# The last norm before the experts: its factors applied to the queries' scores, the queries fed from the unscaled residual

## The reference, cut to what matters

```python
h = h + hybrid_mixer(...)                      # ends in a product with w_out_2
hn = rms_norm(h, ffn_norm_2)                   # h * rsqrt(mean(h*h) + 1e-6) * gain
q = (hn @ w_query).reshape(t, 8, 2, 128)       # 8 heads, two halves of 128
scores = einsum('thcd,hckd->thck', q, sub_keys)
top_s, top_i = top_k(scores, 16)               # then the 16 best sums of 16 x 16, softmax as gates
# experts: gelu(hn . expert_down[idx]), gated, times expert_up[idx]
```

## Time and profile before

| | |
|---|---|
| time of three executions | 3069.96, 3070.07, 3074.51 us; median 3070.07 |
| the profiled execution | 3074.27 us, span 3071.2 us |
| PE busy | 3027.9 us (99%) |
| DVE busy | 2314.5 us (75%) |
| ACT busy | 1672.5 us (54%) |
| POOL busy | 476.7 us (16%) |
| mean granted TensorE clock | 0.996 of 2.4 GHz |
| units split by DVE | 1030, mean 1223 ns |

### The profile page before, as it was taken

One profiled execution on the slowest core, in us unless ns is written; L12 is line 12 of the kernel. 1 busy time (PEld: TensorE's weight loads), 2 busy tenths in 40 slices (PEclk: granted clock), 3 DMA queues, 4 the chain that ended last, 5 costly groups with the idle time before them and its releaser, 6 DMA issues.

```text
span 3071.2 us, 44079 instructions
## 1 busy us (share of the span) xinstructions
PE 3027.9 (99%) x17646; PEld 2695.9 (88%) x17646; DVE 2314.5 (75%) x3465; ACT 1672.5 (54%) x2469; POOL 476.7 (16%) x316
## 2 busy tenths in 40 slices
PE   8999999999999999999999999999999999999999
PEld 7999988888888888889897789999999988888887
DVE  5477667777776455567766589999998898999987
ACT  5454555444444345454564545599975555555544
POOL 1000000000000000000000000133323323775551
PEclk9999999999999999999999999999999999999999
DMA  6543455556555655655344656788889999999997
GB/s 219 187 159 124 143 166 178 186 186 187 186 188 188 197 189 189 188 171 175 117 138 145 202 173 218 256 287 294 287 312 352 357 353 354 402 396 383 392 382 261
DMA packets 199211, 726.79 MB, mean 237 GB/s; under 512 B 22240, under 2 KB 22368, under 8 KB 198496
## 3 DMA queue, kind: packets, MB, share of 16 engines
q1 hardware_dynamic: 161280, 585.44, 56.1%
q0 software_dynamic: 37360, 136.79, 12.2%
q10 hardware_dynamic: 368, 1.75, 0.2%
HBM read 719.24 MB, written 4.19 MB: 236 GB/s over the span
## 4 chain that ended last, share of the span: by engine, by line
PE 91%; DVE 5%; DMA 2%; ACT 2%; issue 1%; ACTq 0%; SPq 0%; DVEq 0%
PE b L2097 90%; DVE wlo L1253 2%; DMA raw<-in_dn 2%; PE b L2105 1%; DVE ar L1242 1%; ACT oh L629 1%; ACT ar L629 0%; ACT whi L633 0%; DVE ar L1831 0%; DVE ar L1823 0%; DVE ar L1818 0%; DVE ar L1815 0%; DVE ar L1826 0%; DMA hsb<-in_x 0%; DVE hsb L2005 0%
## 5 line engine op out<-in xcount | busy, mean ns | idle before, releaser
L1253 DVE TENSOR_TENSOR wlo<-raw,whi 128x1024 fp32r<-128x1024 f32 x1030 | 1252.4, 1223 | 498.5 <-ACT whi L633 494.3
L2097 PE MATMUL b<-aa,whi 128*128 128x256 f32 (+2 forms) x6080 | 1614.2, 343 | 3.7 <-DVE wlo L1253 3.7
L633 ACT ACTIVATE whi<-raw 128x1024 fp32r<-128x1024 f32 x1030 | 1076.3, 1055 | 680.1 <-DMA raw<-in_up 182.1
L2097 PE MATMUL b<-aa,wlo 128*128 128x256 f32 (+1 forms) x4896 | 1280.1, 269 | 0.0
L2097 PEld LDWEIGHTS b<-aa,whi 128*128 128x128 f32 x6080 | 1056.1, 190 | 85.2 <-issue 13.6
L2097 PEld LDWEIGHTS b<-aa,wlo 128*128 128x128 f32 x4896 | 929.7, 190 | 9.8
L2097 PE MATMUL b<-whi,asb 128*128 128x512 f32 x1092 | 366.2, 389 | 2.2 <-DVE ex L1242 2.2
L2097 PE MATMUL b<-whi,aa 128*128 128x512 f32 x1024 | 324.7, 394 | 5.6 <-DVE aa L1250 3.7
L619 POOL DMA_INDIRECT aaf<-in_up,ex x128 | 271.2, 2119 | 161.3 <-DVE aaf L1250 157.9
L2097 PE MATMUL b<-wlo,asb 128*128 128x512 f32 x728 | 283.2, 389 | 0.0
L608 POOL DMA_INDIRECT hsb<-in_dnr,ex x128 | 183.3, 1432 | 464.8 <-DVE small L2005 454.7
(11 more groups left out here) (183 smaller groups left out, 2707.0 us busy)
## 6 DMA issues: line engine op xcount, KB each, us to landing
raw<-in_dn SPq DMA_DIRECT2D x256, 512.0 KB
raw<-in_up SPq DMA_DIRECT2D x182, 512.0 KB
raw<-in_wgu SPq DMA_DIRECT2D x176, 512.0 KB
raw<-in_wdn SPq DMA_DIRECT2D x88, 512.0 KB
raw<-in_w1fm SPq DMA_DIRECT2D x74, 512.0 KB
raw<-in_w2fm SPq DMA_DIRECT2D x74, 512.0 KB
raw<-in_wo SPq DMA_DIRECT2D x64, 512.0 KB
hsb<-in_up SPq DMA_DIRECT2D x44, 512.0 KB, 7.4
```

The source lines that it names most:

```text
L633: return e.activation(o, i, ACT.Copy)
L1253: return e.tensor_tensor(o, a, high.bitcast(F32), ALU.subtract)
L2097: return e.matmul(o, l, r, start=start, stop=stop)
```

## The change

The early flips, highs and lows of the unscaled residual go behind units of the last half of `WO2`, into arrays `PARTS` of their own; the other four groups stand between `WO2` and `WQ`. The last four squares, the factors, the scaling into `XN`, its transposes and its split become a task `renorm` that runs in the ticks of `WQ` and writes `AH`, `AL` for tokens 64 to 255 alone. The factors are applied when ACT copies the scores, as two instructions of 256 columns with a scale in place of one of 512. The queries' scores use two PSUM banks in place of four. The load of `GR` is issued at the end of the task.

The diff, eight columns of indent cut, with the body of the three removed `norm()` left out:

```diff
--- before.py
+++ after.py
@@ -183,7 +183,8 @@
-TURNED = [[4, 5, 6, 7, 4, 5, 6, 7], [6, 7, 5, 1, 2, 0, 3, 4], [4, 5, 6, 7, 0, 1, 2, 3], [0, 1, 2, 3, 4, 5, 6, 7]]
+TURNED = [[4, 5, 6, 7, 4, 5, 6, 7], [6, 7, 5, 1, 2, 0, 3, 4], [4, 5, 6, 7, 0, 1, 2, 3], [0, 1, 2, 3, 4, 5, 6, 7],
+  [5, 6, 7, 3, 5, 6, 7, 3]]
@@ -374,7 +375,8 @@
-    GR = AGf[0:64, 10240:12288]
+    GR = AGf[0:64, 0:2048]
+    JK5 = AGf[:, 3584:4096]
@@ -410,6 +412,16 @@
+with ExitStack() as ph:
+    q15, _, qa, _, qb = [sb(f"parts{i}", n, FR, ph) for i, n in enumerate((3584, 6656, 5632, 8704, 2048))]
+    PARTS = [a[:, i * 512:(i + 1) * 512] for a, n in ((qa, 11), (qb, 4)) for i in range(n)] + [q15[:, 3072:3584]]
+    PARTS = [a.rearrange("p (s t) -> p s t", s=2) for a in PARTS]
+def parts(m, k):
+    return PARTS[k] if m == 4 else AA[:, :, k, :]
@@ -426,6 +438,8 @@
+w_x, w_y, w_p, w_ah, w_al = [sem(f"w_{k}") for k in ("x", "y", "p", "ah", "al")]
@@ -663,7 +677,7 @@
-            act(AH[:, k, :], B[TURNED[m][g]][:, (k % 2) * 256:(k % 2) * 256 + 256], ACT.Copy,
+            act(parts(m, k)[:, 0, :], B[TURNED[m][g]][:, (k % 2) * 256:(k % 2) * 256 + 256], ACT.Copy,
@@ -685,26 +699,33 @@
-    def norm():
+    def renorm():
+        for i, (t, c) in enumerate(((0, 2), (1, 2), (0, 3), (1, 3))):
+            e.wait_ge(s_add, 40)
+            e.wait_ge(n_sq, 36 + i)
+            square(JK5, h[:, t, hcol(c)], t, c).then_inc(n_sq, 1)
+            if i % 2:
+                yield
...
+        yield
+        for n in range(25):
+            c, g = n // 6, n // 3 - 1
+            if n % 6 == 0 and c < 4:
+                e.wait_ge(n_v, NV[4] + 6)
+                if c == 3:
+                    e.wait_ge(w_p, 2)
+                act(XN[:, c % 3, 1, :], h[:, 1, hcol(c)], ACT.Copy, scale=small[:, 13:14]).then_inc(w_y, 1)
+            if n % 3 == 0 and g >= 0:
+                e.wait_ge(w_p, g + 1)
+                e.wait_ge(s_u, U["WQ"])
+                for k in (2 * g, 2 * g + 1):
+                    o = (k % 2) * 256
+                    act(AH[:, k, TS:256], B[6 + g % 2][:, o + TS:o + 256], ACT.Copy,
+                        scale=col(GAIN[4], k)).then_inc(w_ah, 1)
+            yield
+        e.wait_ge(s_sk, 16)
+        e.wait_ge(w_p, 8)
+        e.dma_start(GR, g5).then_inc(s_sk, 16)
@@ -1106,14 +1127,15 @@
-         lambda ch, t, c, u: add_h(33 + 4 * ch + 2 * c + t, t, 2 * ch + c, B[BANKS[15 + ch][2 * c + t]]))
+         lambda ch, t, c, u: None if ch else add_h(33 + 2 * c + t, t, c, JK5),
+         lambda ch, n: high(4, n - 7) if ch and 7 <= n < 11 else None)
-    e.wait_ge(n_sq, 40)
-    e.dma_start(GR, g5).then_inc(s_sk, 16)
-    norm()
+    for g in range(4, 8):
+        high(4, g)
+    tasks.add(renorm())
@@ -1121,7 +1143,11 @@
-        cp(SCS[:, :, hd * 256:(hd + 1) * 256], B[4 + hd % 4].rearrange("p (t w) -> p t w", t=2)).then_inc(s_sc, 1)
+        e.wait_ge(n_v, NV[4] + 6)
+        for t in range(2):
+            last = act(SCS[:, t, hd * 256:(hd + 1) * 256], B[4 + hd % 2][:, t * 256:(t + 1) * 256], ACT.Copy,
+                       scale=small[:, 12 + t:13 + t])
+        last.then_inc(s_sc, 1)
@@ -1291,8 +1317,9 @@
-            stt(AL[:, k, :], B[bank][:, (k % 2) * 256:(k % 2) * 256 + 256], col(GAIN[m], k),
-                AH[:, k, :].bitcast(F32), ALU.mult, ALU.subtract).then_inc(n_al, 1)
+            p = parts(m, k)
+            stt(p[:, 1, :], B[bank][:, (k % 2) * 256:(k % 2) * 256 + 256], col(GAIN[m], k),
+                p[:, 0, :].bitcast(F32), ALU.mult, ALU.subtract).then_inc(n_al, 1)
@@ -1310,23 +1337,25 @@
-    def norm():
+    def renorm():
+        yield
+        yield
...
+        yield
+        for n in range(25):
+            c, g = n // 6, n // 3 - 1
+            if n % 6 == 0 and c < 4:
+                e.wait_ge(n_v, NV[4] + 6)
+                if c == 3:
+                    e.wait_ge(w_p, 2)
+                ts(XN[:, c % 3, 0, :], h[:, 0, hcol(c)], small[:, 12:13], None, ALU.mult).then_inc(w_x, 1)
+            if n % 3 == 0 and g >= 0:
+                e.wait_ge(w_ah, 2 * g + 2)
+                for k in (2 * g, 2 * g + 1):
+                    o = (k % 2) * 256
+                    stt(AL[:, k, TS:256], B[6 + g % 2][:, o + TS:o + 256], col(GAIN[4], k),
+                        AH[:, k, TS:256].bitcast(F32), ALU.mult, ALU.subtract).then_inc(w_al, 1)
+            yield
@@ -1794,11 +1823,14 @@
-    rows(U["WO2"] + 8, order2[4:16], 2, tasks, need2, unit, lambda ch, t, c, u: add(15 + ch, t, 2 * ch + c, u))
+    rows(U["WO2"] + 8, order2[4:16], 2, tasks, need2, unit, lambda ch, t, c, u: add(15 + ch, t, 2 * ch + c, u),
+         lambda ch, n: low_parts(4, n - 7) if ch and 7 <= n < 11 else None)
-    norm()
+    for g in range(4, 8):
+        low_parts(4, g)
+    tasks.add(renorm())
@@ -1878,7 +1910,7 @@
-    e.wait_ge(n_a, 14)
+    e.wait_ge(w_y, 4)
@@ -2119,8 +2151,12 @@
+        elif m == 3:
+            e.wait_ge(s_pv, 8 if g < 4 else 12 if g < 6 else 16)
-            e.wait_ge(s_pv, 8 if g < 4 else 12 if g < 6 else 16)
+            e.wait_ge(s_add, 36 if g < 4 else 38 if g < 6 else 40)
+            if g >= 4:
+                e.wait_ge(n_al, 64 + 2 * g - 6)
@@ -2138,17 +2174,23 @@
-    def norm():
...
+    def renorm():
+        for n in range(27):
+            g = (n - 5) // 3
+            if n >= 5 and n % 3 == 2:
+                if g % 2 == 0:
+                    e.wait_ge(w_x, g // 2 + 1)
+                    e.wait_ge(w_y, g // 2 + 1)
+                e.wait_ge(n_al, 80)
+                if g >= 2:
+                    e.wait_ge(w_al, 2 * g - 2)
+                for k in (2 * g, 2 * g + 1):
+                    for t in range(2):
+                        o = (k % 2) * 256 + t * 128
+                        last = tr(B[6 + g % 2][:, o:o + 128],
+                                  XN[:, g // 2 % 3, t, (k % 4) * 128:(k % 4 + 1) * 128])
+                last.then_inc(w_p, 1)
+            yield
@@ -2176,11 +2218,12 @@
+                p = parts(m, k)
-                    mm(b, hi, AA[:, :, k, :], k == 0, False)
-                last = mm(b[:, 0:256], lo, AH[:, k, :], False, False)
+                    mm(b, hi, p, k == 0, False)
+                last = mm(b[:, 0:256], lo, p[:, 0, :], False, False)
-                    last = mm(b, hi, AA[:, :, k, :], False, True)
+                    last = mm(b, hi, p, False, True)
@@ -2560,28 +2603,32 @@
-                      lambda ch, j, n=n: wo2_free(8 * n + 4 * ch + j)), nothing)
+                      lambda ch, j, n=n: wo2_free(8 * n + 4 * ch + j)), nothing,
+             early(4, 4) if n else None)
-    norm()
+    for g in range(4, 8):
+        flip(4, g)
+    tasks.add(renorm())
-        e.wait_ge(s_sk, 32)
+        e.wait_ge(s_sk, 16)
-        if hd >= 4:
-            e.wait_ge(s_sc, hd - 3)
+        if hd >= 2:
+            e.wait_ge(s_sc, hd - 1)
-                last = mm(B[4 + hd % 4][:, (2 * t + c) * 128:(2 * t + c + 1) * 128],
+                last = mm(B[4 + hd % 2][:, (2 * t + c) * 128:(2 * t + c + 1) * 128],
-             fm_unit(lambda i: i % 4, lambda i: (s_sum, S["WQ"] + i // 2 - 1) if i >= 4 else (n_al, 66), 4),
+             fm_unit(lambda i: i % 4, lambda i: (s_sum, S["WQ"] + i // 2 - 1) if i >= 4 else
+                     {0: (s_add, 40), 3: (n_al, 80)}.get(i), 4),
@@ -2617,6 +2664,8 @@
+        if u == U["D"]:
+            e.wait_ge(w_al, 16)
```

More of the change, by code:

```diff
@@ L686, in stats @@
                 yield
-            def norm():
-                power(4, 8)
[L690 to L707, removed]
+            def renorm():
[5 more added lines that the diff above has]
+                        yield
+                power(4, 8)
+                yield
[17 more added lines that the diff above has]
+                e.dma_start(GR, g5).then_inc(s_sk, 16)
             def rs_rows(o, w, mean, wait, a, n, scale=1.0):
@@ L2139, in spread @@
                 yield
-            def norm():
-                for g in range(8):
-                    c = g // 2
-                    if g % 2 == 0:
-                        e.wait_ge(n_v, NV[4] + 7 + c)
-                        e.wait_ge(n_a, 8 + 3 + c)
-                    for k in (2 * g, 2 * g + 1):
-                        for t in range(2):
-                            o = (k % 2) * 256 + t * 128
-                            last = tr(B[g][:, o:o + 128], XN[:, c % 3, t, (k % 4) * 128:(k % 4 + 1) * 128])
-                    last.then_inc(n_p, 1)
+            def renorm():
[15 more added lines that the diff above has]
+                    yield
             def plain_unit(bank, free):
```

## The result

| | before | after |
|---|---|---|
| measured with the prediction, median | 3070.2 us (7 runs, 3069.49 to 3075.4) | 3063.01 us (7 runs, 3058.67 to 3065.74) |
| ratio, 95% interval | | 0.997 [0.996, 0.998] |
| the profiled execution: time, span | 3074.27, 3071.2 | 3058.67, 3056.9 |
| executions with a span on record (before: without the seven of the first row): count, mean time | 99, 3072.12 | 21, 3064.81 |
| the same: mean span | 3069.04 | 3063.06 |

The kernel became faster by 0.2 to 0.4%; the means differ by 7.3 us, of which 6.0 lie inside the span (5.5 by the medians of the spans) and 1.33 outside it. The profiled execution of after was the fastest of its kernel's 21, so the 14.3 us between the two profiled spans are not the effect.

The account below looks back on a forecast made before the run. PE was taken to bound until DVE's last wait in the queries' stage, DVE after it: 11.65 - 1.6 - 2.4 = 7.65, less 1.4 is 6.3 us, from the 3070.07 median to 3063.8 us; range 3061.5 to 3069.5.

Parts of the forecast that it names:

- DVE does not absorb: Rival: the periods of `WQ` have no room, all DVE's new work counts, 7.2 us; gain 2.9, time 3067.2; chance 0.15.
- starved weights: Rival: the burst of loads and stores delays the weights, 2.5 us of PE's wait; gain 3.8, time 3066.3; chance 0.10.
- the clock falls: Rival: sixteen transposes between `WO2` and `WQ` run slow, 2.1 us back; gain 4.2, time 3065.9; chance 0.04.
- The boundary: Between `WO2` and `WQ`: PE's gap of 13.85 us shrinks to 2.2, saving 11.65 us.
- Early flips: Sixteen transposes behind two units of the last half of `WO2`: 1.6 us added on PE, 0 on ACT and DVE.
- The second turning: Eight groups of four transposes in `WQ`: six cost PE 0.40 us each, 2.4; the last two cost DVE 1.4.
- DVE absorbs until the last third: In `WQ`: DVE's idle 2.1 us per four units takes up its 1.8 of new work, up to unit 23.
- the wait in `sink_q`: DVE's wait in the queries' stage, 2.10 us before: shorter, 1 us or less, but still present behind unit 23.
- The clock: Between `WO2` and `WQ`: granted clock of 1.00 after the change, transposes keeping it up, against the skill's rule.
- `GR`, the burst, the highs: Costs of 0: `GR` has 18 us to land, 3.15 MB of DMA traffic fits 6.6 us of slack, splits are in time.
- `GR` late: Rival: DVE waits for the `GR` load behind `WQ`; at three times its duration 12.6 us slower, 3082.7; chance 0.05.
- DVE's addition is hidden: Rival: PE, not DVE, bounds the end of `WQ`; gain 6.85, time 3063.2; chance 0.17.

Follow-up runs that it names:

- no_second: The changed kernel without the second turning (scaling, transposes and split of `renorm` left out; output not the reference's): 3061.45 us, ratio 0.9964 to the kernel before.
- gap_warm: The kernel before with 56 transposes of the identity, result unread, where PE would have waited behind `WO2`: 3072.22 us, ratio 0.9996.
- dense: The changed kernel with a group of the second turning every second tick, not every third: 3065.89 us, ratio 0.9976 to the kernel before.
- twice_early: The changed kernel with the twelve lows of groups 0 to 5, ahead of DVE's last wait, done twice: 3063.96 us, one run.
- twice_late: The changed kernel with the four lows of groups 6 and 7, behind DVE's last wait, done twice: 3068.52 us, one run.

## Why the prediction was off

I forecast 3063.8 us with "within 0.2%" a hair (0.48 to 0.47) ahead of "faster". The kernels measured together gave 3063.01, and the gain of 7.3 us is beyond 0.2% (6.1 us). Inside the span the mechanism was right and the sum 0.7 too high; what failed is the step that turned a gain of the span into one of the time. The 6.0 us inside the span alone would have been just within 0.2%; with what changed outside it the gain is beyond. That 3063.8 came so near 3063.01 is in part luck: the sum too high by 0.7 and the 1.33 left out pull in opposite directions. And my own sum of 6.3 was already past 6.1: "within" was ahead only by the rivals "DVE does not absorb", "starved weights" and "the clock falls" (0.29 together), none of which came.

- **What lies around the span: the step that failed.** I took the sum, a gain of the span, off the profiled execution's time and off the median as they stood, as if the 3074.27 - 3071.2 = 3.07 us outside the span stayed. They became 1.75: over 99 executions of before they were 3.08 on average and wandered from 2.03 to 5.41, over 21 of after never outside 1.70 to 1.81. That is 1.33 us, a fifth of the gain. Every variant of the changed kernel but one shows 1.75; no_second shows 1.89 and gap_warm 2.08. So it does not go by the work: gap_warm does the work of before and 56 instructions more, and still has less outside its span. Its cause was not found, and no row from before the result shows it.
- **The boundary**: 11.65 us said, 12.05 in the profiled pair, 11.9 on the mean of six profiles of before. The last adds hid behind the first transposes: 2.02 us from matmul to matmul, where my 2.2 us, counted from 0.23 behind the last start, make 2.4.
- **Early flips**: 1.6 said, 1.82 measured.
- **The second turning**: the term of the sum that was mis-sized. I had 6 groups x 0.40 = 2.4 on PE and 1.4 on DVE, 3.8 in all; measured 3.18 and 1.31, 4.49 in all. So the split at DVE's last wait was right, and the 1.4 nearly so; the price of a group was 3.18 / 6 = 0.53, not 0.40. In dense's timeline the group itself takes 1757.30 - 1756.94 = 0.36 us and the matmul behind it lasts 0.48 in place of 0.40; the rest, near 0.1, is spread over the matmuls that follow, whose starts are up to 0.01 us further apart than in no_second.
- **DVE absorbs until the last third**: right (twice_early 0.00, twice_late +1.73). But one sign was off: I had said that the wait in `sink_q` would be 1 us or less, and the last one is 1.65. A low of 192 columns is 0.37 us where I had 0.34.
- **The clock**: right that it stays at 1.00. The Trainium skill (TensorE: Matmul & The Clock Gate, Part 4: PE-mode transpose) says that transposes do not count as PE work for the gate. The 56 transposes of gap_warm, with the clock at 1.00 where the kernel before waited and fell to 0.50, do not agree with it. The boundary is no test: its transposes last 2 us, and in the kernel before the clock was still 0.93 over the first 4 us without any work. Of the old gap 0.6 us hung on the half clock, by gap_warm.
- **`GR`, the burst, the highs**: costs of 0, all held: 7.3 us for `GR`, a PE busy for 4.00 of 4.00 us at 433 GB/s, lows in time for unit 1.
- **The rivals**: "DVE does not absorb", "starved weights", "the clock falls" and "`GR` late" are refuted by the same rows. "DVE's addition is hidden" was close in its total, 6.85, for the wrong reason: late additions do count.

Together: 11.9 - 1.82 - 4.49 = 5.6 us local; with the 1.33 outside it is 6.9, and the 0.4 that remain of 7.3 are within what the rest of the program wanders.

## What to carry to other kernels

Measure a small change between two marks of one engine on either side of it: here the one around the change repeated within 0.3 us, most to hundredths, where whole executions differ by 5 and more, and it shows which segments repeat and which wander. A norm's factors can be applied behind the product, so the product need not wait for the norm; the price is a second, scaled copy for those who need it scaled, and it should be done while the other engines still wait for PE. Price a short insertion by what it does to the instructions behind it, not by its own length, and look at the time outside the span as well as at the span.

## What the runs showed of the hardware

- Between matmuls of 128 rows, a group of four transposes of which two have 64 rows (`64*128 64x64` in the trace) and two 128 takes 1.08 us from matmul to matmul, one of four with 128 rows 0.60. A group of four with 128 rows costs the stage 0.53 us, more than its own 0.36.
- Transposes alone held the granted clock at 1.00 (56 in a row, 6.3 us). What the half clock after a wait of PE costs depends on who sets the time: 0.6 us in the old gap, which another chain bounded, though sixteen transposes were 1.7 us longer in it; 1.6 to 2.7 us behind the wait in `WO2`, where PE bounds.
- The time outside the span was constant to 0.1 us for one program and spread over 3.4 us for its near twin.
